# Low parts of the weights: a GpSimd subtraction replaced by a negated copy and an adding transfer

## The reference, cut to what matters

```python
h = h + y
h = h + sq_relu_mlp(rmsnorm(h, norm_mlp_g[i]), mlp_w1[i], mlp_w2[i])
# sq_relu_mlp:  jnp.square(jax.nn.relu(h @ w1)) @ w2
# dsa_mixer:    proj = h @ w_in ... o.reshape(b, length, D_MODEL) @ w_out
# conv_mixer:   a = h @ w_pw1 + b_pw1 ... u @ w_pw2 + b_pw2
```

## Time and profile before

| | us |
|---|---|
| median of three runs | 1785.44 |
| profiled execution, first to last instruction (span) | 1783.3 |
| TensorE busy with matmuls | 1765.0 |
| GpSimd busy | 788.2 |
| of it, the 286 subtractions | 707.7 |
| ScalarE busy | 740.4 |
| of it, the 286 roundings | 300.8 |
| VectorE busy | 824.1 |
| share of the 16 DMA engines for the loads' queue | 30.5% |

### The profile page before, as it was taken

How to read it: one execution, slowest core, us unless ns; L and a number is a source line. 1 busy time by engine, 2 the same in 40 slices (tenths; PEclk the granted TensorE clock), 3 DMA queues, 4 the chain that set the end, 5 groups by cost and what they waited for, 6 DMA issues and landing times.

```text
span 1783.3 us, 20517 instructions
## 1 busy us (share of the span) xinstructions
PE 1765.0 (99%) x8105; PEld 1448.6 (81%) x8105; DVE 824.1 (46%) x1326; ACT 740.4 (42%) x1160; POOL 788.2 (44%) x351
## 2 busy tenths in 40 slices
PE   9999999999999999999999999999999999999998
PEld 7888778888888878888888888887777888888787
DVE  4794553310121189942210121177867851359843
ACT  5533444321232244554322232365545542445542
POOL 4343224554444469934444444444544544344221
PEclk9999999999999999999999999999999999999999
DMA  6232212333333323223333333343333233242111
GB/s 208 73 104 78 60 48 73 101 110 94 95 99 102 90 86 97 83 60 95 95 96 104 97 95 95 94 130 93 88 92 95 83 107 95 68 117 77 62 60 47
DMA packets 108544, 162.51 MB, mean 91 GB/s; under 512 B 12352, under 2 KB 38592, under 8 KB 108448
## 3 DMA queue, kind: packets, MB, share of 16 engines
q1 hardware_dynamic: 108448, 161.20, 30.5%
HBM read 157.51 MB, written 2.10 MB: 90 GB/s over the span
## 4 chain that ended last, share of the span: by engine, by line
PE 94%; DVE 3%; ACT 1%; DMA 1%; issue 0%; SPq 0%; DVEq 0%; ACTq 0%
PE bank L670 28%; PE bank L672 28%; PE bank L671 28%; PE bank L997 2%; PE bank L941 1%; PE bank L871 1%; PE bank L756 1%; PE bank L853 1%; PE bank L1156 1%; PE bank L861 0%; DMA residual<-in_x 0%; PE bank L1141 0%; DVE gla_r L2427 0%; PE bank L1151 0%; PE bank L967 0%
## 5 line engine op out<-in xcount | busy, mean ns | idle before, releaser
L2588 POOL TENSOR_TENSOR w_lo<-w_raw,w_hi 128x1024 fp32r<-128x1024 f32 (+1 forms) x286 | 707.7, 2479 | 948.2 <-ACT w_hi L1247 948.2
L1247 ACT ACTIVATE w_hi<-w_raw 128x1024 fp32r<-128x1024 f32 (+1 forms) x286 | 300.8, 1055 | 570.2 <-PE bank L672 563.4
L670 PE MATMUL bank<-x_hi,w_hi 128*128 128x512 f32 (+1 forms) x1264 | 503.2, 398 | 0.3 <-DVE x_lo L2372 0.3
L672 PE MATMUL bank<-x_hi,w_lo 128*128 128x512 f32 (+1 forms) x1264 | 492.5, 390 | 0.0
L671 PE MATMUL bank<-x_lo,w_hi 128*128 128x512 f32 (+1 forms) x1264 | 492.0, 389 | 0.0
L670 PEld LDWEIGHTS bank<-x_hi,w_hi 128*128 128x128 f32 (+1 forms) x1264 | 236.8, 187 | 54.3 <-issue 5.5
L671 PEld LDWEIGHTS bank<-x_lo,w_hi 128*128 128x128 f32 (+1 forms) x1264 | 236.9, 187 | 53.6 <-issue 4.8
L672 PEld LDWEIGHTS bank<-x_hi,w_lo 128*128 128x128 f32 (+1 forms) x1264 | 236.7, 187 | 50.6
L670 PE MATMUL bank<-w_hi,f_hi 128*128 128x512 f32 x512 | 200.0, 391 | 0.0
L672 PE MATMUL bank<-w_hi,f_lo 128*128 128x512 f32 x512 | 199.3, 389 | 0.0
L671 PE MATMUL bank<-w_lo,f_hi 128*128 128x512 f32 x512 | 199.3, 389 | 0.0
(11 more groups left out here) (332 smaller groups left out, 2096.4 us busy)
## 6 DMA issues: line engine op xcount, KB each, us to landing
w_raw<-in_mlp_w SPq DMA_DIRECT2D x128, 512.0 KB, 3.8
w_raw<-in_even_w_in SPq DMA_DIRECT2D x48, 512.0 KB, 3.7
w_raw<-in_dsa_w_in SPq DMA_DIRECT2D x28, 512.0 KB, 3.7
w_raw<-in_odd_w_in SPq DMA_DIRECT2D x24, 512.0 KB, 3.7
w_raw<-in_conv_w_pw SPq DMA_DIRECT2D x32, 256.0 KB, 3.0
w_raw<-in_even_w_out SPq DMA_DIRECT2D x16, 512.0 KB, 3.8
w_raw<-in_dsa_w_out SPq DMA_DIRECT2D x8, 512.0 KB, 3.8
w_raw<-in_conv_w_pw SPq DMA_DIRECT2D x8, 512.0 KB, 3.9
```

Of the source, the lines that this page charges most:

```text
L670: e.matmul(o, sh, mh, start=first, stop=False)
L672: m = e.matmul(o, sl, mh, start=False, stop=last)
L1247: e.activation(hi, src, ACT.Copy).then_inc(*w_hi.up(u))
L2588: e.tensor_tensor(lo, src, hi.bitcast(F32), ALU.subtract).then_inc(*w_lo.up(u))
```

## The change

ScalarE writes two tiles for each unit: the rounded weights into `w_hi`, and the rounded weights negated into the slot of `w_lo`. GpSimd no longer subtracts. It issues a transfer from its own queue that adds the raw tile to what stands in `w_lo`. The landing of that transfer is what TensorE and SyncE now wait for, by one semaphore for each slot of the ring. Three semaphores of VectorE are merged into others, since the chip has a limited number.

```diff
-        w_hi = signal("w_hi_rounded", every_unit)
-        w_lo = signal("w_lo_split", every_unit)
+        w_neg = signal("w_hi_negated", every_unit)
+        w_low = [signal(f"w_lo_landed{i}", every_unit[i::RING], 16) for i in range(RING)]
...
+        def low_of(u):
+            return w_low[u % RING].at(u)
...
-        gains = signal("gains_made", ["final_even"])
-        eps_set = signal("eps_set", ["zero", "eps", "lags"])
+        eps_set = signal("eps_set_then_gains_made", ["zero", "eps", "lags", "final_even"])
...
@@ TensorE, by_features, by_tokens and tile_by_tile
-                            w.wait_ge(*w_lo.at(u))
+                            w.wait_ge(*low_of(u))
...
@@ ScalarE, split_to
-                    e.activation(hi, src, ACT.Copy).then_inc(*w_hi.up(u))
+                    e.activation(hi, src, ACT.Copy)
+                    e.activation(lo, src, ACT.Copy, scale=-1.0).then_inc(*w_neg.up(u))
...
@@ GpSimd, split_to
-                    w.wait_ge(*w_hi.at(u))
-                    e.tensor_tensor(lo, src, hi.bitcast(F32), ALU.subtract).then_inc(*w_lo.up(u))
+                    w.wait_ge(*w_neg.at(u))
+                    e.dma_start(lo.bitcast(F32), src, accum_op=ALU.add).then_inc(*w_low[u % RING].up(u))
...
@@ SyncE, load_to
-                        w.wait_ge(*w_lo.at(u - RAW))
+                        w.wait_ge(*low_of(u - RAW))
```

More of the change, by code:

```diff
@@ L621, in build @@
         k_gla = signal("gla_k_scaled", range(4))
-        wg_zero = signal("wg_zeroed", ["zero"])
-        lr_out = signal("lr_scaled_then_low_parts", ["lr", "w_lo", "lr_lo"])
+        lr_out = signal("wg_zeroed_then_lr_scaled_then_low_parts", ["zero", "lr", "w_lo", "lr_lo"])
         z_mm = signal("z_product", HEAD_DIRS)
@@ L1242, in split_to @@
                     u = split[0]
-                    src, hi, _ = ring(u)
+                    src, hi, lo = ring(u)
                     w.wait_ge(*raw_in[u % RAW].at(u, len(units[u].parts) - 1))
@@ L1261, in round_x @@
                 w.wait_ge(*turned.at(n, k))
-                w.wait_ge(*gains.last())
+                w.wait_ge(*eps_set.last())
                 if x_free is not None:
@@ L1279, in take_root @@
             def take_root(n):
-                w.wait_ge(*eps_set.last())
+                w.wait_ge(*eps_set.at("lags"))
                 w.wait_ge(*stat_sum.at(n))
@@ L1867, in vector_program @@
             e.tensor_tensor(final_even[:, :], V("final_g", 0, KD), V("even_g", 0, KD),
-                            ALU.mult).then_inc(*gains.up("final_even"))
+                            ALU.mult).then_inc(*eps_set.up("final_even"))
             for k in range(KD):
@@ L2382, in vector_program @@
             diagonals(4, stat(5, 2))
-            e.memset(wg, 0.0).then_inc(*wg_zero.up("zero"))
+            e.memset(wg, 0.0).then_inc(*lr_out.up("zero"))
             for j, b in enumerate(HIGH):
@@ L2584, in split_to @@
                     u = split[0]
-                    src, hi, lo = ring(u)
+                    src, _, lo = ring(u)
                     w.wait_ge(*raw_in[u % RAW].at(u, len(units[u].parts) - 1))
-                    w.wait_ge(*w_hi.at(u))
-                    e.tensor_tensor(lo, src, hi.bitcast(F32), ALU.subtract).then_inc(*w_lo.up(u))
+                    w.wait_ge(*w_neg.at(u))
+                    e.dma_start(lo.bitcast(F32), src, accum_op=ALU.add).then_inc(*w_low[u % RING].up(u))
                     split[0] += 1
@@ L2810, in sync_program @@
             up_to("gq")
-            w.wait_ge(*wg_zero.last())
+            w.wait_ge(*lr_out.at("zero"))
             e.dma_start(head_g[:, :], a["gla_norm_g"].partition_broadcast(P)).then_inc(*head_in.up("row"))
```

## The result

The changed kernel takes 1813.78 us (median of four runs, 1812.14 to 1814.9), the kernel before beside it 1785.31. The ratio is 1.0157, with a 95% interval from 1.0145 to 1.0169. The profiled execution has a span of 1811.0 us, 27.7 more than before; the predicted time was 1807, in a range from 1790 to 1910.

A forecast was written before the change was run, and what follows sets the result against it. The prediction took TensorE's own work as the bound, busy 1765.0 of 1783.3 us. Terms of 21.0 us, plus 2.1 around the profiled span, gave 1783.3 + 21.0 + 2.1 = 1806.4, said as 1807, range 1790 to 1910.

The forecast's parts named there:

- the rival with the lower clock: TensorE's clock falls after three new waits of 4 to 5 us, some 2 us each: 1813 us; chance 0.1.
- the thin places: Start, pw1 products, eout_b1 and oout1, where TensorE comes to a unit sooner; the thinnest margin, at two places, 0.2 us.
- A: Time from the end of ScalarE's second rounding to TensorE's start on the unit: 6.5 us, bounds 2.6 and 9.9.
- The tile-by-tile products: eout_b1 and oout1, which run through all four ring units every 5.44 us: 4.7 us lost at each.
- the start: First weight units: unit 1 ready 3.4 us late, plus 0.5 for busy DMA engines, 3.9 us lost.
- pw1: The convolution's pw1 products: one unit 1.2 us late, five more groups 0.3 each, 1.5 in all.
- the reload that waits for the landing still has more than ten: Dense stretches: SyncE's reload of a raw buffer keeps over ten us to spare, so nothing is lost.
- ScalarE's terms: Negations ahead of chains: 2.0 us at gla_v, 1.0 at gla_state, 2.0 for softmax attention and the boundary after eout_b1.
- the third rival: Faster: GpSimd leaves VectorE's path, shortening chains for prob and gla_state; needs A under 2.6 us, at most 7 us; chance 0.02.
- The DMA engines: Rival: adding transfers make them the bound in dense stretches from 3.67 us a unit, 1850 to 2200 us; chance 0.20.
- The rule against the change: VectorE in a two-port mode blocks GpSimd's descriptor writes: A grows by some 0.7 us at four places, 3 us more.

The follow-up runs named there:

- e3: The changed kernel with a plain copy from GpSimd's queue in place of the adding transfer: 1789.35 us, 1.0019 to the kernel before.
- e4: The changed kernel with 34 of the 286 units, those at the thin places, done as before: 1783.04 us, 0.9983 to the kernel before.
- e1: The changed kernel with SyncE's queue reordered, issuing two other groups of transfers ahead of two raw loads each: 1799.24 us, 1.0074 to the kernel before.
- e10: The kernel before in all but five units (32 to 35 and 273), which get negation and adding transfer: 1779.78 us, 0.9965.
- e2: The changed kernel with GpSimd adding raw to ScalarE's negative by a tensor_tensor instruction, no transfers: 1801.15 us, 1.0083 to the kernel before.
- e8: e2 with its first 13 units as in the kernel before, without negation: 1794.47 us, 1.0051 to the kernel before.
- e5: e4 with 20 more units, 17 to 36, done as before: 1785.86 us, 1.0 to the kernel before.
- e6: The changed kernel with 30 more transposes where TensorE stands idle at the start: 1810.79 us, 1.0139 to the kernel before.
- e7: e4 with nine more units done as before (195, 196, 203, 204, 223, 224, 271 to 273): 1783.28 us, 0.9987 to the kernel before.

## Why the prediction was right, and where it was not

**The time and the sign.** 1813.78 us against 1807, slower as forecast. That the time came so close is luck: the sum left out 19 us that came (SyncE's queue 9.4, the clock 9.7), and its named terms, 21.0, came to 8.6 with the small ones at the gates. The 1813 of the rival with the lower clock is nearer still by the same cancelling. What held is the mechanism at the thin places. (TensorE's waits before add up to 12.0 us, not 13; nothing hangs on it.)

**A.** 6.5 us predicted, 6.41 measured. Its parts were off: the transfer takes 5.8 for the 5.3 assumed, the issue 0.6 for 1.2. The argument that an adding transfer costs two passes held in kind: e3 shows a ratio of 2.2 in engine time.

**The tile-by-tile products and the start.** 4.7, 4.7 and 3.9 us against 4.3, 3.2 and 3.6. e4 took the transfers from these units, among others, and the three waits went. Reading the thin places row by row worked. At the start it was unit 0, not unit 1, that TensorE waited for: its landing came 8.0 us after its negation, among the crowded loads, and unit 1 was then in time.

**pw1.** 2.7 us predicted, 0.5 measured. The unit of the earlier trace rows landed 5.1 us after its negation, not 6.5, and 1.1 us in time; one of the six groups was late. At margins of about an us the scatter of A decides, and a single value can't forecast it.

**The step that failed, though the time did not show it: "the reload that waits for the landing still has more than ten" us.** That looked at weights only. SyncE's wait has slack for the reload itself, but the prediction never named what stands behind it in SyncE's queue. With that cover gone at two places the price was 9.4 us, and 4.2 more by the clock. e1 undid exactly this and got 14.5 us back.

**The clock.** Named as a rival, at 2 us each for three waits. It came at five waits, for 1.4 to 2.8 us each. With three waits in the forecast longer than any in the trace, it belonged in the sum and not among the rivals. "The clock never fell" holds for the trace of before, and perhaps not for each of its runs: of the 49 beside the experiments, the 15 with a mean granted clock of 1.000 took 1784.9 us on average, the 34 with less took 1786.1.

**ScalarE's terms.** 5 us, in the attentions, were forecast as losses. The kernel after gained 3.1 and 1.6 there instead (`gla_v` and `gla_state` together), because the third rival, GpSimd out of VectorE's path, was at work at the same places. It was given 0.02 and the condition that A be small, as if it excluded the losses; it adds to them. Its bound of 7 us was right: e10 gains 5.0 us at the two places in its trace, and 6.7 in the medians. The 1.7 between may be short falls of the clock behind these waits in runs of the kernel before; no trace here shows that. The prediction said of L2233, 0.67 to 2.89 us, that nobody waits for it. True of that line; its maximum after:

```profile
L2235 DVE TENSOR_TENSOR rg_i<-rg_i,rg_t x16: 664/685/693, 1242.6 to 1418.8; 128x512 f32<-128x512 f32 x16
```

What was missed is that the same stretching stood in the chains for which TensorE waits, at `prob` (1.65 us for 384 columns) and at `gla_middle` (2.18 us for four).

**The DMA engines.** Not the bound, as forecast, by a margin of 0.7 us a unit. The whole share is 0.75, and 0.86 in the dense stretch, nearer to the limit than the predicted 0.6.

**The rule against the change,** that VectorE keeps GpSimd from writing descriptors, does not show in the issues: the 286 take 0.85 to 1.21 us, the middle one 0.86. Whether it is a part of what scatters the landings is not shown.

What stays open: e2's loss is only partly assigned. e8 shows that the early negations are 5.8 to 6.7 us of it (against the kernel before beside each, and by the medians), and e3, apart from what its late start may hide, that they cost this only beside GpSimd's instruction; the other pieces were not taken apart one by one. The landings scatter between 3.9 and 9.7 us, and a good part of that goes with the loads beside them: in the quarter of the units where the loads' packets took none of the engines' time in the first 3.9 us after the issue, the middle landing came after 5.1 us, and in the quarter where they took most of it, 2.5 us, after 7.0. No run was made to test it.

## What to carry to other kernels

When a step becomes later but stays off the critical path, look at every queue that waits for it and list what else stands in that queue behind the wait: there, not at the step itself, half of this loss arose. A wait of over 3 us of TensorE cost its length and, in 9 of 11 cases here, a stretch of half clock on top. And before moving a whole stream of work from one engine to another, look for the few instructions of it that hold up a chain: five units of 286 had nearly all the gain.

## What the runs showed of the hardware

- An adding transfer of 512 KB within SBUF, issued from GpSimd, lands after 5.8 us and takes 2.93 us of all 16 DMA engines; a plain copy of the same tile lands after 3.1 and takes 1.33. GpSimd is busy 870 ns issuing the one, 535 ns the other.
- Some instructions of VectorE that meet a GpSimd tensor_tensor end only when it has ended: 2.19 us for 0.17 of work, 1.65 for 0.42. It depends on the form. Of those that started during a subtraction in the kernel before, 36 of 42 tensor_tensor with all inputs in SBUF took longer than their shortest like; of 26 with one input in a bank, where TensorE writes, none did, nor of the 45 MAX8 and MATCH_REPLACE8, which work on SBUF alone.
- After a wait TensorE's clock may fall to half for 3.4 or 6.8 us. In the traces of this case it did in 9 of 11 waits of 3.1 to 5.4 us and in 6 of 13 of 2.1 to 2.9 us; behind the same 2.2 us for `gla_v` it fell in e1 and e4 and stayed in the kernel after, e2, e3, e5, e6 and e8. After one of 1.6 us it fell once (e7), where 0.7 more followed. In the trace of the kernel before the longest was 1.54, also with 0.7 behind it, and it stayed.
